# The choice of 128 keys made for fewer tokens, in four tiles counted from token 80

## The reference, cut to what matters

```
s_idx = relu(einsum('bqhd,bkd->bqhk', qi, k_idx))      # 8 index heads
score = einsum('bqh,bqhk->bqk', wi, s_idx)
adm   = cid[None, :] <= qc[:, None]                    # cid: chunk of a key, qc: chunk of the token
score = where(adm, score, -inf)
_, sel = top_k(score, topk)                            # topk = min(256, 512 // 4) = 128
valid  = cid[sel] <= qc
logits = where(valid, q . kv[sel] * scale, -1e30)
```

## Time and profile before

| | us |
|---|---|
| median of 3 runs | 2532.1 |
| lowest and highest | 2530.58, 2538.29 |
| the profiled execution | 2536.86 |
| its span, first to last instruction | 2535.0 |
| mean granted TensorE clock | 0.945 |
| busy: PE, PEld, DVE, ACT, POOL | 2269.7, 1533.8, 983.3, 454.6, 86.2 |

### The profile page before, as it was taken

How to read it: one execution, slowest core, us unless ns; L and a number is a source line. 1 busy time by engine, 2 the same in 40 slices (tenths; PEclk the granted TensorE clock), 3 DMA queues, 4 the chain that set the end, 5 groups by cost and what they waited for, 6 DMA issues and landing times.

```text
span 2535.0 us, 26124 instructions
## 1 busy us (share of the span) xinstructions
PE 2269.7 (90%) x10017; PEld 1533.8 (61%) x10017; DVE 983.3 (39%) x1982; ACT 454.6 (18%) x855; POOL 86.2 (3%) x116
## 2 busy tenths in 40 slices
PE   7999999988988999999899997788899688878886
PEld 5888888335753888887648774456785432222232
DVE  5454533232662645542530217876652400000014
ACT  2010000253361000101220014433113100000001
POOL 0000000000001000000110000000000000000000
PEclk9999999999999999999999997789999798899898
DMA  4232221211003322321142210000242399999996
GB/s 131 67 100 67 96 92 57 86 50 34 1 1 108 126 84 83 100 100 63 46 105 75 74 42 1 1 9 1 75 141 95 154 407 427 426 426 427 427 395 282
DMA packets 175750, 347.45 MB, mean 137 GB/s; under 512 B 18004, under 2 KB 146644, under 8 KB 155170
## 3 DMA queue, kind: packets, MB, share of 16 engines
q1 hardware_dynamic: 169504, 331.22, 35.3%
q0 software_dynamic: 5536, 12.71, 1.3%
q10 hardware_dynamic: 610, 2.17, 0.2%
HBM read 337.50 MB, written 16.45 MB: 140 GB/s over the span
## 4 chain that ended last, share of the span: by engine, by line
PE 69%; DMA 16%; DVE 7%; ACT 3%; DVEq 2%; issue 2%; SPq 0%; ACTq 0%; PEldq 0%; PEld 0%
PE PS L612 17%; DMA M<-w 11%; PE PS L643 10%; PE PS L3018 7%; PE PS L69 7%; PE PS L2367 5%; DMA M<-w_ffn_up 4%; PE PS L386 4%; PE PS L2549 2%; PE PS L924 2%; PE PS L1632 1%; PE PS L904 1%; DVE M L1958 1%; PE PS L988 1%; PE PS L1153 1%
## 5 line engine op out<-in xcount | busy, mean ns | idle before, releaser
L612 PE MATMUL PS<-M 128*128 128x256 f32 x2464 | 541.0, 382 | 16.9 <-DVE M L357 12.2
L612 PEld LDWEIGHTS PS<-M 128*128 128x128 f32 x2464 | 468.7, 191 | 90.1 <-issue 13.8
L3018 PE MATMUL PS<-M 128*64 128x512 f32 x1536 | 369.7, 642 | 81.2 <-DMA M<-w 58.1
L3018 PEld LDWEIGHTS PS<-M 128*64 128x64 f32 x1536 | 115.1, 148 | 323.4 <-issue 226.5
L643 PE MATMUL PS<-M 128*128 128x256 f32 x1232 | 268.7, 379 | 4.5 <-DVE M L731 2.5
L643 PEld LDWEIGHTS PS<-M 128*128 128x128 f32 x1232 | 233.4, 190 | 41.6 <-issue 10.3
L69 PE MATMUL PS<-M 128*128 128x264 f32 (+1 forms) x774 | 186.9, 402 | 16.5 <-DVE M L1701 5.4
L69 PEld LDWEIGHTS PS<-M 128*128 128x128 f32 x774 | 147.3, 193 | 55.2 <-issue 13.2
L3108 DVE TENSOR_TENSOR M<-M,PS 128x512 f32<-128x512 f32 x16 | 11.0, 688 | 413.9 <-PE PS L3018 413.9
L734 DVE TENSOR_TENSOR M<-M,PS 128x256 f32<-128x256 f32 x220 | 92.6, 421 | 200.3 <-PE PS L612 196.3
L2367 PE MATMUL PS<-M 128*128 128x264 f32 x616 | 141.8, 392 | 8.0 <-DVE M L2466 5.0
(11 more groups left out here) (391 smaller groups left out, 2312.2 us busy)
## 6 DMA issues: line engine op xcount, KB each, us to landing
M<-w SPq DMA_DIRECT2D x128, 1024.0 KB, 19.8
M<-w SPq DMA_DIRECT2D x32, 2048.0 KB, 23.8
M<-w_ffn_gate SPq DMA_DIRECT2D x22, 1024.0 KB, 5.5
M<-w_ffn_up SPq DMA_DIRECT2D x22, 1024.0 KB, 5.3
M<-w_ffn_down SPq DMA_DIRECT2D x16, 1024.0 KB, 5.1
M<-w_in SPq DMA_DIRECT2D x13, 1024.0 KB, 5.3
M<-w_in SPq DMA_DIRECT2D x25, 512.0 KB, 3.8
M<-w_ffn_down SPq DMA_DIRECT2D x8, 768.0 KB, 4.7
```

The source lines that it names most:

```text
L612: last = nc.tensor.matmul(PS[:, 3 * half + BANK[p], 0:HALF], lhs[:, a, :], rhs[:, a, :], start=p in FIRST and a == 0, stop=p in LAST and a ...
L3018: last = nc.tensor.matmul(PS[ROWS * k:ROWS * k + ROWS, bank, :], wide[:, a * P + ROWS * k:a * P + ROWS * k + ROWS], weights(k), start=star ...
```

## The change

The choice is made for tokens 80 to 527 only, in four tiles: 80 to 207, 208 to 335, 336 to 463, and 64 tokens, 464 to 527. They look at 208, 336, 464 and 528 keys. The results lie in buffers of their own (`CHOSEN`), and SP moves their rows to the attention's tiles in `MB` (`masks_sp`, 11 DMAs from SBUF to SBUF, in SP's list behind the loads of the first gate unit). The rows of tokens 0 to 79 are written by one operation without a choice, and three small memsets fill the keys that the moved rows don't reach. The copies to `QTAIL` go. `masked` waits for 6 transfers ahead of its first unit and for the 5 of the last tile ahead of unit 24. One semaphore (`y_zeroed`) is merged into another (`y_st`), whose counts move by 16.

```diff
-KEYS = (144, 272, 400, S2, S2)
+UNCUT = META + 64
+CHOICE_TILES = [(UNCUT, 128), (UNCUT + 128, 128), (UNCUT + 256, 128), (UNCUT + 384, 64)]
+KEYS = tuple(lo + w for lo, w in CHOICE_TILES)
...
-            pool.wait_ge(r_out, 12)
-            for i in range(4):
-                nc.gpsimd.tensor_copy(QTAIL[:, i, :].rearrange("p (m r) -> p m r", m=4), over(QI[:, i, TAIL0:S2], 4))
...
-                    q = QI[rows, pair, j * P:(j + 1) * P] if j < 4 else QTAIL[rows, pair, :]
-                    last = nc.tensor.matmul(PS[:, 6 + k, 0:w], q, KI[rows, lo:lo + w], start=True, stop=True)
+                    last = nc.tensor.matmul(PS[0:m, 6 + k, 0:w], QI[rows, pair, first:first + m], KI[rows, lo:lo + w],
+                                            start=True, stop=True)
...
-            for j in range(5):
-                keys = KEYS[j]
-                sc, wk, nb = MB[:, j, 0:keys], WK[:, 0:keys], NB[:, 0:keys]
+            for j in range(NQ):
+                m, keys = CHOICE_TILES[j][1], KEYS[j]
+                sc, wk, nb, m8 = CHOSEN[j][0:m], WK[0:m, 0:keys], NB[0:m, 0:keys], M8[0:m]
...
+        def masks_sp(sp):
+            for s in range(NQ):
+                sp.wait_ge(choice_made, s + 1)
+                head = P - UNCUT
+                if s < 3:
+                    sp.dma_start(MB[UNCUT:P, s, 0:KEYS[s] - UNCUT + 16], CHOSEN[s][0:head, 0:KEYS[s] - UNCUT + 16]
+                                 ).then_inc(masks_in, 16)
+                    sp.dma_start(MB[0:UNCUT, s + 1, 0:KEYS[s]], CHOSEN[s][head:P]).then_inc(masks_in, 16)
+                else:
+                    sp.dma_start(MB[UNCUT:P, s, :], CHOSEN[s][0:head]).then_inc(tail_masks_in, 16)
+                    for m in range(4):
+                        sp.dma_start(MB[32 * m:32 * m + 32, 4, :], CHOSEN[s][32:64]).then_inc(tail_masks_in, 16)
...
+            nc.vector.tensor_scalar(MB[0:UNCUT, 0, 0:META + P], cidk[0:UNCUT, 0:META + P], C["cidq"][0:UNCUT, NQ:NQ + 1], -BIG,
+                                    ALU.is_gt, ALU.mult)
+            for s in range(3):
+                nc.vector.memset(MB[0:UNCUT, s + 1, KEYS[s]:KEYS[s] + UNCUT - META], -BIG)
...
+                if n == 0:
+                    dve.wait_ge(masks_in, 16 * 6)
+                if n == 24:
+                    dve.wait_ge(tail_masks_in, 16 * 5)
...
                 sp.dma_start(slot(s, 2048, 4, 2 * P), wcols(("w_up_a_2", "w_up_b_2")[side], 2 * P * i, 2 * P)
                              ).then_inc(w_ready[s], 16)
+                if n == 0:
+                    masks_sp(sp)
...
-                    act.wait_ge(x_acc, 36)
+                    act.wait_ge(x_acc, 2 * max(n for n in range(4 * NQ) if n % 3 == 2) + 2)
```

More of the change, by code:

```diff
@@ L179, in constants @@
     c["c_cidk"] = np.tile(cid[None, :S2], (P, 1))
-    c["c_cidq"] = cid.reshape(5, P).T.copy()
-    c["c_cidq"][:, 4] = cid[TAIL0 + p % 32]
+    c["c_cidq"] = np.stack([cid[lo + p % w] for lo, w in CHOICE_TILES] + [cid[p]], axis=1)
     c["c_bd16"] = (p[:, None] // 16 == np.arange(8)[None, :]).astype(f)
@@ L1636, in proj2_pe @@
                 pe.drain().then_inc(w_used[s], 1)
-            for t in range(5):
+            for t, (lo, w) in enumerate(CHOICE_TILES):
                 k = after("pe", v2_free)
@@ L1641, in proj2_pe @@
                     pe.wait_ge(ck_out, 1)
[L1642 to L1645, removed]
+                nc.tensor.matmul(PS[0:w, 2 + (k - 1) % 2, 0:8], WIT[:, lo:lo + w], ident[0:8, 0:8], start=True,
+                                 stop=True).then_inc(v2_ready, 1)
             pe.wait_ge(tails_set, 2)
@@ L1683, in proj2_act @@
             jobs = [(w, VA[0:w, t, 256 * c:256 * c + 256], 256) for c in range(2) for t, (lo, w) in enumerate(TOK_TILES)]
-            jobs += [(P, WI[:, t, :], 8) for t in range(5)]
+            jobs += [(w, WI[0:w, t, :], 8) for t, (lo, w) in enumerate(CHOICE_TILES)]
             jobs += [(w, (VB[0:w, t, :] if t < 5 else VBD), S1) for t, (lhsT, w) in enumerate(V_TILES)]
@@ L1727, in program @@
         WK, NB, M8 = at(WORK0, S2), at(WORK0 + 528, S2), at(WORK0 + 18360, 8)
+        CHOSEN = [at(SCR + 7700 + sum(KEYS[:s]), KEYS[s]) for s in range(len(KEYS))]
+        choice_made, masks_in, tail_masks_in = sems("choice_made", "masks_in", "tail_masks_in")
+        NQ = len(CHOICE_TILES)
         x_s, x_r, x_acc = sems("x_s", "x_r", "x_acc")
@@ L1763, in select_step @@
             return int(STEPS * (sum(OP_COST[:j]) + OP_COST[j] * op / TILE_OPS) / sum(OP_COST))
-        CHUNKS = [(j, pair, c) for j in range(5) for pair in range(4) for c in range(1 if KEYS[j] <= 512 else 2)]
+        CHUNKS = [(j, pair, c) for j in range(NQ) for pair in range(4) for c in range(1 if KEYS[j] <= 512 else 2)]
         def chunk_keys(j, c):
@@ L1874, in scores @@
                     pe.wait_ge(x_r, c)
+                first, m = CHOICE_TILES[j]
                 for k in range(2):
                     rows = slice(64 * k, 64 * k + 64)
-                    q = QI[rows, pair, j * P:(j + 1) * P] if j < 4 else QTAIL[rows, pair, :]
-                    last = nc.tensor.matmul(PS[:, 6 + k, 0:w], q, KI[rows, lo:lo + w], start=True, stop=True)
+                    last = nc.tensor.matmul(PS[0:m, 6 + k, 0:w], QI[rows, pair, first:first + m], KI[rows, lo:lo + w],
+                                            start=True, stop=True)
                 last.then_inc(x_s, 1)
@@ L1921, in positive @@
                     act.wait_ge(x_acc, 2 * n - 4)
-                nc.scalar.activation(RL[n % 3][:, :, lo:lo + w], PS[:, 6:8, 0:w], ACT.Relu).then_inc(x_r, 1)
+                m = CHOICE_TILES[j][1]
+                nc.scalar.activation(RL[n % 3][0:m, :, lo:lo + w], PS[0:m, 6:8, 0:w], ACT.Relu).then_inc(x_r, 1)
             nc.scalar.preload_act_table_set(LN_EXP)
@@ L1940, in select_dve @@
         def select_dve(dve):
-            for j in range(5):
-                keys = KEYS[j]
-                sc, wk, nb = MB[:, j, 0:keys], WK[:, 0:keys], NB[:, 0:keys]
+            for j in range(NQ):
+                m, keys = CHOICE_TILES[j][1], KEYS[j]
+                sc, wk, nb, m8 = CHOSEN[j][0:m], WK[0:m, 0:keys], NB[0:m, 0:keys], M8[0:m]
                 yield select_step(j, 0)
-                nc.vector.tensor_scalar(nb, cidk[:, 0:keys], C["cidq"][:, j:j + 1], -BIG, ALU.is_gt, ALU.mult)
+                nc.vector.tensor_scalar(nb, cidk[0:m, 0:keys], C["cidq"][0:m, j:j + 1], -BIG, ALU.is_gt, ALU.mult)
                 dve.drain()
@@ L1951, in select_dve @@
                     dve.wait_ge(x_r, sum(1 for cj, pair, _ in CHUNKS if 4 * cj + pair <= n))
-                    nc.vector.scalar_tensor_tensor(sc, RL[n % 3][:, h % 2, 0:keys], WI[:, j, h:h + 1], nb if h == 0 else sc,
-                                                   ALU.mult, ALU.add).then_inc(x_acc, 1)
+                    nc.vector.scalar_tensor_tensor(sc, RL[n % 3][0:m, h % 2, 0:keys], WI[0:m, j, h:h + 1],
+                                                   nb if h == 0 else sc, ALU.mult, ALU.add).then_inc(x_acc, 1)
                     dve.drain()
@@ L1957, in select_dve @@
                     yield select_step(j, 9 + 2 * r)
-                    nc.vector.max(M8, src)
+                    nc.vector.max(m8, src)
                     dve.drain()
                     yield select_step(j, 10 + 2 * r)
-                    nc.vector.match_replace(out=wk, in_to_replace=M8, in_values=src, imm_value=-3e38)
+                    nc.vector.match_replace(out=wk, in_to_replace=m8, in_values=src, imm_value=-3e38)
                     dve.drain()
@@ L1966, in select_dve @@
                 yield select_step(j, 42)
-                nc.vector.scalar_tensor_tensor(MB[:, j, 0:keys], wk, -BIG, nb, ALU.mult, ALU.add)
+                nc.vector.scalar_tensor_tensor(sc, wk, -BIG, nb, ALU.mult, ALU.add).then_inc(choice_made, 1)
                 dve.drain()
+        def masks_sp(sp):
[10 more added lines that the diff above has]
+                        sp.dma_start(MB[32 * m:32 * m + 32, 4, :], CHOSEN[s][32:64]).then_inc(tail_masks_in, 16)
         def stick_dve(dve):
@@ L2745, in program @@
         comb_in, frs, fout = [sem(f"comb_in{t}") for t in range(5)], sem("frs"), sem("fout")
-        gfin_in, rows_stored, y_zeroed = sems("gfin_in", "rows_stored", "y_zeroed")
+        gfin_in, rows_stored = sems("gfin_in", "rows_stored")
         hsum = sem("hsum")
@@ L2754, in zero_rows_pool @@
             pool.dma_start(y_dram.rearrange("(c r) (k d) -> (r k) c d", r=32, k=4),
-                           ZERO.unsqueeze(1).to_broadcast([P, 2 * S2 // 32, D // 4])).then_inc(y_zeroed, 16)
-            pool.wait_ge(y_zeroed, 16)
+                           ZERO.unsqueeze(1).to_broadcast([P, 2 * S2 // 32, D // 4])).then_inc(y_st, 16)
+            pool.wait_ge(y_st, 16)
         def route_sp(sp):
@@ L3001, in experts_pool @@
             scatter_rows(pool, rest + (BASE - 3))
-            pool.wait_ge(y_st, rest * 16 + 16 * (BASE - 2))
+            pool.wait_ge(y_st, rest * 16 + 16 * (BASE - 1))
             pool.sem_inc(rows_stored, 1)
```

(2 more changed lines are left out.)

3 lines of the change are left out of this document (1 added, 2 removed).

## The result

The changed kernel took 2521.6 us (median of 5 runs, 2519.7 to 2524.3); the kernel before, run again beside it, 2536.8 (2530.6 to 2538.3). The ratio is 0.9947, 95% interval 0.9933 to 0.9961, which is 13 us less; the two medians lie 15 us apart. Forecast were 20 us less, 2512 us with a range of 2503 to 2524. The profiled execution took 2524.3 us, its span is 2522.5 against 2535.0.

The account below looks back on a forecast made before the run. The prediction took VectorE (DVE) to bound the 20 soft-sum units: 118 us of its order plus 18 of waits, 136 for 156, and 0.3 elsewhere, rounded to 20 us. So 2532.1 - 20 = 2512 us, range 2503 to 2524.

Parts of the forecast that it names:

- What bounds the kernel now: In the 20 soft-sum units (156.1 us), DVE sets the pace, mostly with the choice; PE's 118 us prove no second bound.
- VectorE's order: DVE's operations up to the last soft sum: 129.4 us of choice and 12.7 of soft sums, 142 us before, 118 after.
- The cost of a tile, what is removed: DVE's choice: 17.9 us a tile at 144 keys, 35.1 at 528; one tile and 336 keys go, 26.6 us.
- The table of the Trainium skill's "VectorE: DVE Perf Modes": SBUF-to-SBUF operations on DVE cost 58 + columns cycles at 0.96 GHz; it would make the removed work 17.6 us.
- What of it is on the path: Choice ahead of the last soft sum shrinks by 24.1 us, from 129.4 to 105.3; it ends 9.7 us behind that sum.
- What is late next: In the 20 units, 118 us of DVE's order plus 18 of waits give 136 us for 156, a gain of 20.
- p: Share of PE's matmuls in the units at the low clock level: 0.30, held after the change, giving 110.8 us of PE.
- Rival 2: PE binds the units at the low level: p 0.4, 120 us of PE, 147 us, gain 9, 2523 us; chance 0.18.
- Rival 1: Clock rises with denser work in the units: waits 8 us for 14, gain 30, 2502 us; chance 0.13.
- The rule named beside that rival: On PE's clock gate, the throttled state is the default and activity releases it; by it the clock would rise.
- The other parts: Around the units: one index-weight job less gives 0.2 to 0.4 us; added DVE operations nothing or 0.8; masks 30 us to spare.

Follow-up runs that it names:

- g1: Kernel before with score chunks spread over the units, a unit's first chunk ahead of z and its relu ahead of the softplus: 2534.5 us, ratio 0.9992.
- g4: Kernel before with 5 dummy matmuls ahead of each wait for the relu of a chunk of the same unit: 2540.7 us, ratio 1.0018.
- f3: Changed kernel with score chunks spread over the units, a unit's first chunk ahead of z and its relu ahead of the softplus: 2503.7 us.
- f1: Changed kernel with the 20 chunks of scores spread over the units, mostly one to a unit: 2508.4 us, ratio to before 0.9893.
- f2: Changed kernel with a unit's first chunk of scores ahead of z and its relu ahead of the softplus: 2504.8 us, ratio to before 0.9876.
- f4: Changed kernel with 5 dummy matmuls ahead of each wait for the relu of a chunk of the same unit: 2510.2 us, ratio to before 0.9894.
- e1: Changed kernel with dummy matmuls, 4 ahead of the exponential wait and 6 ahead of the last chunk's relu wait: 2520.6 us, ratio to before 0.9939.
- e2: Kernel before with dummy matmuls, 4 ahead of the exponential wait and 6 ahead of the last chunk's relu wait: 2551.9 us, ratio 1.0065.

## Why the prediction came out as it did

- *What bounds the kernel now*: right for the kernel before, where neither g1 nor g4 got below VectorE's order, and only half read. That PE waited 2.6 us for DVE was taken as a sign of DVE's pace. It was also a sign of how little room PE's list had, 6.5 us with all its gaps.
- *The cost of a tile, what is removed*: right. VectorE's busy time fell by 19.9 us in the units and 2.3 behind them, the rounds lie on the line, 64 partitions cost 0.70 us for 0.71. The table of the Trainium skill's "VectorE: DVE Perf Modes" (section on the TRN2 errata), set beside that row in the prediction, would have had the rounds at 528 columns at 0.61 us; the kernel after has 0.70.
- *What of it is on the path*: 24.1 us of VectorE's order were ahead of the last sum, and the choice ended 9.5 us behind it (9.7 forecast). That they are worth 24 us once VectorE is the bound on both sides is seen in f3 against g1. In the changed kernel as it was built only 9.6 us came off, since TensorE's list was the bound.
- *What is late next*: the step that failed, by its size. The term was 18 us of waits; it measured 29.2. The forecast held the low-level share at p = 0.30 and took a PE that is 83% busy (110.8 of 136 us are 81%) to have the rest to spare; its waits for the relu and the exponential, 31.5 us in the rows of the kernel before, were in no sum. Its own matmuls took 119.0 / 480 = 0.248 us each, so p = 0.39. With p held, PE's list would have been 110.8 + 12.8 + 13.5 = 137 us, near the 136 forecast; 8.2 of the 10.4 us missed are the growth of p.
- *Rival 2* (p = 0.4, 120 us of PE, units of 147 us) had 0.18 and is what came about, in its number: 146.4. The range of 2503 to 2524 holds 2521.6 because it took in the near side of this rival; the forecast's own 2507 to 2517 does not, and its cause, VectorE's pace, is not what set the time. That the range holds the time is luck as far as the forecast's own account goes. The condition named against the rival, that p grew only if lulls grew, was not met: PE's idle time in front of `later`, the scores, `z` and `values` shrank, from 2.6 + 17.6 + 13.9 + 0.7 = 34.8 us to 13.5 + 12.8 + 0.7 = 27.0, while its time at the low level, 2 x (1 - clock) of the units, went from some 69 to some 79 us. The share hangs on where PE stands: in f1, f2 and f4, where the stops in front of a chunk are fewer or filled, p is 0.25, 0.23 and 0.13. Why it grew from the kernel before to the changed one no run takes apart.
- *Rival 1*, the clock rising with denser work, was wrong: PE was busy 81% of the units for 76%, and the level fell from 0.78 to 0.73. The lulls came from the order of the lists, and stayed. The rule named beside that rival, from the Trainium skill's "TensorE: Matmul & The Clock Gate" ("What's actually happening"), agrees with e1, f4 and g4, in which more activity in the lulls brought the level up to 0.91 to 0.95. The kernels before and after do not bear it out in the way the rival used it, by the busy share of the whole stretch.
- *The other parts*: one job of the index weights gave 0.4 us, the four operations fit in the gap ahead of the first sum (1.74 us of it left), and the masks came with 35 us to spare, all as forecast.
- *Not in the sum*: 2.9 us in the early gate and 1.4 in the attention, whose clocks were 1.00 and 1.00 for 0.84 and 0.98, and 2.4 us the other way ahead of the first sum (2.8 in stages that were not touched, less the 0.4). With the 9.6 of the units and 1.0 of the rest this is the 12.5 of the profiled executions. The median of before itself moved from 2532.1 to 2536.8 with two more runs.

## What to carry to other kernels

When two engines feed each other, add up each one's own list, busy time and waits for third engines together. What a cut in the first can give is the room that the second list has and what the change takes off that list itself: here 6.5 us of room and 4.3 us off the list (149.6 to 145.3), of which 9.6 came, for 24 us taken off VectorE. A chunk that waits for an activation queued behind another stage's activations costs twice, once as a wait and once as the clock behind it. Here it paid to put it where the engine waits anyway (15.6 to 20.9 us of the units), or to fill the lull with a few dummies (14.5 us for 130 of them); many dummies in a full list gave 2.6 us (356 in e1) or cost 12.7 (452 in e2).

## What the runs showed of the hardware that was not expected

An operation of VectorE with two operands in SBUF stood while POOL added two operands in SBUF. L1964 at 208 columns took 1.25 us, where 0.375 is due by an estimate on the line between its 0.308 us at 144 columns and its 0.709 at 528. Timeline of the changed kernel, POOL and DVE:

```profile
1561.10 1.33 POOL L1791 TENSOR_TENSOR M<-M 128x544 f32<-128x544 f32 x1 [5.51 <-PE PS L1843]
1561.41 1.25 DVE L1964 TENSOR_TENSOR M<-M 128x208 f32<-128x208 f32 x1
```

VectorE's ends 0.2 us behind POOL's, as if it had stood until POOL was done. A weighted sum in g1 did the same, 1.51 us at 272 columns for 0.50 in the kernel before, and 0.3 us behind POOL's end, and so did one in g4. It goes the other way as well: in the kernel before, VectorE was first, and POOL's operation, 0.24 us elsewhere, took 0.62 and ended 0.1 us behind VectorE's.

```profile
1554.97 1.33 POOL L1793 TENSOR_TENSOR M<-M 128x544 f32<-128x544 f32 x1 [4.48 <-PE PS L1845]
1555.09 1.51 DVE L1958 SCALAR_TENSOR_TENSOR M<-M 128x272 f32<-128x272 f32 x1
...
1653.17 0.71 DVE L1964 TENSOR_TENSOR M<-M 128x528 f32<-128x528 f32 x1
1653.36 0.62 POOL L1793 TENSOR_TENSOR M<-M 16x32 f32<-16x32 f32 x1 [12.22 <-PE PS L1837]
```

The rounds of `max`, with one operand, show no such step (0.64 us at 464 columns beside a POOL operation in f1), nor does a soft sum with one of its two operands in PSUM (0.72 us there). The Trainium skill's "SBUF — State Buffer" ("SBUF: two separate sides") has a port that VectorE and GpSimd share and that one of them holds for a whole instruction; these rows agree with it. No experiment was made on it.
